# Feed-forward gate and up: one 512-column and one 256-column matmul in place of three of 256

## The reference

```python
D_MODEL, D_FF, SEQ = 1024, 2816, 256
for layer in range(2):
    h = rms_norm_3(x, ffn1_norm[layer])
    x = x + FFN_RES * swiglu(h, ffn1_w_gate[layer], ffn1_w_up[layer], ffn1_w_down[layer])
    ...   # pooling and convolution, or selected attention
    h = rms_norm_3(x, ffn2_norm[layer])
    x = x + FFN_RES * swiglu(h, ffn2_w_gate[layer], ffn2_w_up[layer], ffn2_w_down[layer])
# swiglu(h, g, u, d) = (silu(h @ g) * (h @ u)) @ d
```

## Time and profile before

| | us |
|---|---|
| median of 3 runs | 2860.81 |
| lowest, highest | 2857.11, 2861.9 |
| span of the profiled execution | 2859.0 |

### The profile page before, as it was taken

The page is one execution under the profiler, slowest core; times in us unless marked ns, Lnnn a source line. Parts: engine busy times, 40 slices in busy tenths (PEclk is TensorE's granted clock), DMA queues, the critical chain, the costliest instruction groups (busy, mean ns, idle before and its releaser), DMA issues. The chain is left out here.

```text
span 2859.0 us, 34779 instructions
## 1 busy us (share of the span) xinstructions
PE 2528.2 (88%) x14785; PEld 1811.3 (63%) x14785; DVE 1213.7 (42%) x1891; ACT 936.4 (33%) x1495; POOL 36.9 (1%) x51
## 2 busy tenths in 40 slices
PE   9898787767998889867978999999889999988998
PEld 7642222227742233217867777998779899887997
DVE  6520000026622000015665565655765565566654
ACT  5420000016510000013444434544544454434543
POOL 0010000000010000000000000000000000001000
PEclk9999999988999999998998999999999999999999
DMA  7099999993299999998222434555235555544452
GB/s 268 20 428 428 424 427 428 428 390 115 78 421 424 426 426 426 428 355 229 89 89 96 162 133 163 164 182 191 94 118 179 190 178 189 172 150 144 150 180 78
DMA packets 229162, 690.43 MB, mean 241 GB/s; under 512 B 35953, under 2 KB 135233, under 8 KB 205328
## 3 DMA queue, kind: packets, MB, share of 16 engines
q1 hardware_dynamic: 227728, 685.06, 64.0%
q0 software_dynamic: 1280, 3.15, 0.4%
HBM read 687.09 MB, written 5.28 MB: 242 GB/s over the span
## 5 line engine op out<-in xcount | busy, mean ns | idle before, releaser
L520 PE MATMUL accumulators<-xT_halves,weight_highs 128*128 128x256 f32 (+1 forms) x4400 | 812.7, 287 | 18.0 <-PEq L361 15.5
L267 DVE TENSOR_TENSOR weight_lows<-weight_ring,weight_highs 128x1024 fp32r<-128x1024 f32 (+1 forms) x504 | 602.9, 1213 | 435.5 <-ACT weight_highs L258 431.0
L520 PEld LDWEIGHTS accumulators<-xT_halves,weight_highs 128*128 128x128 f32 (+1 forms) x4400 | 693.5, 194 | 26.5 <-DVE weight_lows L267 14.4
L258 ACT CAST weight_highs<-weight_ring 128x1024 fp32r<-128x1024 f32 (+1 forms) x504 | 517.5, 1041 | 443.3 <-PE accumulators L520 424.9
L520 PE MATMUL accumulators<-xT_halves,weight_lows 128*128 128x256 f32 (+1 forms) x2200 | 628.0, 285 | 0.0
L1737 PE MATMUL accumulators<-weight_ring,arena 128*32 128x512 f32 x2048 | 471.8, 622 | 93.0 <-DMA weight_ring<-in_moe_w_up 50.7
L520 PEld LDWEIGHTS accumulators<-xT_halves,weight_lows 128*128 128x128 f32 (+1 forms) x2200 | 426.0, 194 | 0.5
L1737 PEld LDWEIGHTS accumulators<-weight_ring,arena 128*32 128x32 f32 x2048 | 135.6, 114 | 421.1 <-issue 420.9
L520 PE MATMUL accumulators<-weight_highs,arena_halves 128*128 128x512 f32 x1040 | 333.3, 398 | 12.4 <-PEq L361 5.4
L1737 PE MATMUL accumulators<-weight_ring,work 128*32 128x512 f32 x896 | 208.4, 620 | 34.8 <-DMA weight_ring<-in_moe_w_down 24.3
L520 PEld LDWEIGHTS accumulators<-weight_highs,arena_halves 128*128 128x128 f32 x1040 | 199.6, 192 | 57.5 <-issue 12.0
(11 more groups left out here) (441 smaller groups left out, 1970.7 us busy)
## 6 DMA issues: line engine op xcount, KB each, us to landing
weight_ring<-in_moe_w_gate SPq DMA_DIRECT2D x64, 2048.0 KB, 18.7
weight_ring<-in_moe_w_up SPq DMA_DIRECT2D x64, 2048.0 KB, 18.8
weight_ring<-in_moe_w_down SPq DMA_DIRECT2D x56, 2048.0 KB, 18.8
weight_ring<-in_ffn_w_gate SPq DMA_DIRECT2D x44, 1024.0 KB, 5.3
weight_ring<-in_ffn_w_up SPq DMA_DIRECT2D x44, 1024.0 KB, 5.3
weight_ring<-in_ffn_w_down SPq DMA_DIRECT2D x44, 1024.0 KB, 4.9
weight_ring<-in_l_w_in SPq DMA_DIRECT2D x38, 1024.0 KB, 5.1
weight_ring<-in_moe_w_down SPq DMA_DIRECT2D x32, 512.0 KB, 14.0
```

The source lines that it names most:

```text
L258: act.copy(p.high(), p.raw()).then_inc(self.high_ready, 1)
L267: dve.tensor_tensor(p.low(), p.raw(), p.high().bitcast(F32), ALU.subtract).then_inc(self.low_ready, 1)
L520: last = pe.matmul(out, left[a], right[b], start=(start and i == 0), stop=(stop and i == 2), **kw)
```

## The change

A group becomes two matmuls. The high weight tile streams the high and the low tokens in one matmul of 512 columns, into a bank of its own; the low weight tile streams the 256 high tokens into the first half of that bank. The two halves of a bank are then one sum in two parts: ScalarE copies the first half (two banks, 2 x 256 columns) to `gate` or `prod`, and VectorE adds the second half to it, and only then scales, or multiplies. Eight banks are in use in place of four, so TensorE waits in unit 1 for the row factors to have left bank 6, and before the down product for the sum of unit 9. ScalarE's new copies stand ahead of the Silu (gate) and at the end of the turn (up), each behind a wait for TensorE's last use of the part's weights; the cast of piece 4u + 7 moves from the next turn to before the up copy.

```diff
+    def bank(u, part, f):
+        return u % 2 * 4 + part * 2 + f
+
+    def sides(u, part):
+        acc = m.ps[:, bank(u, part, 0):bank(u, part, 0) + 2, :]
+        return acc[:, :, 0:T], acc[:, :, T:2 * T]
+
+    def two(x, u):
+        return x[:, u % 2, :].rearrange("p (f t) -> p f t", f=2)
 # TensorE
                     if u >= 2:
                         if part == 0:
-                            pe.wait_ge(s["scaled"], u - 1)
+                            pe.wait_ge(s["gate_summed"], u - 1)
                         else:
-                            pe.wait_ge(s["hidden"], u - 1)
+                            pe.wait_ge(s["up_summed"], u - 1)
+                    if (u, part) == (1, 1):
+                        pe.wait_ge(s["spread_moved"], 1)
...
                         for f in range(2):
-                            last = three(pe, acc[:, f * T:(f + 1) * T], [x[:, f * P:(f + 1) * P] for x in w], [m.xT_r[:, c, k, :] for k in range(2)],
-                                         f == 0 and c == 0, c == DC - 1, skip_group_check=True)
+                            high, low = (x[:, f * P:(f + 1) * P] for x in w)
+                            acc = m.ps[:, bank(u, part, f), :]
+                            pe.matmul(acc, high, m.xT_r[:, c, :, :].rearrange("p k t -> p (k t)"), start=(c == 0), stop=False, skip_group_check=True)
+                            last = pe.matmul(acc[:, 0:T], low, m.xT_r[:, c, 0, :], start=False, stop=(c == DC - 1), skip_group_check=True)
...
+            pe.wait_ge(s["up_summed"], n - 1)
             for i in range(FFC - 2):
                 out.chunk(pe, i)
 # ScalarE
             for u in range(n):
                 m.highs(act, gs.piece(4 * u + 2 + LEAD))
+                gs.wait_used(act, 2 * u)
+                if u == 0:
+                    act.wait_ge(s["spread"], 1)
+                if u >= 2:
+                    act.wait_ge(s["hidden"], u - 1)
+                act.copy(two(gate, u), sides(u, 0)[0]).then_inc(s["gate_copied"], 1)
                 act.wait_ge(s["scaled"], u + 1)
                 act.activation(gate[:, u % 2, :], gate[:, u % 2, :], ACT.Silu).then_inc(s["silu_out"], 1)
                 if u > 0:
                     rounded(u - 1)
+                m.highs(act, gs.piece(4 * u + 4 + LEAD) - 1)
+                gs.wait_used(act, 2 * u + 1)
+                if u >= 2:
+                    act.wait_ge(s["hidden_low"], u - 1)
+                act.copy(two(prod, u), sides(u, 1)[0]).then_inc(s["up_copied"], 1)
 # VectorE
-                gs.wait_used(dve, 2 * u)
-                dve.tensor_tensor(gate[:, u % 2, :].rearrange("p (j t) -> p j t", j=2), m.ps[:, u % 2 * 2, :].rearrange("p (j t) -> p j t", j=2),
-                                  bview(late.rows_of, 1, 2), ALU.mult).then_inc(s["scaled"], 1)
+                dve.wait_ge(s["gate_copied"], u + 1)
+                dve.tensor_tensor(two(gate, u), sides(u, 0)[1], two(gate, u), ALU.add).then_inc(s["gate_summed"], 1)
+                dve.wait_ge(s["gate_summed"], u + 1)
+                dve.tensor_tensor(two(gate, u), two(gate, u), bview(late.rows_of, 1, 2), ALU.mult).then_inc(s["scaled"], 1)
                 m.lows(dve, gs.piece(4 * u + 4 + LEAD) - 1)
-                gs.wait_used(dve, 2 * u + 1)
+                dve.wait_ge(s["up_copied"], u + 1)
+                dve.tensor_tensor(two(prod, u), sides(u, 1)[1], two(prod, u), ALU.add).then_inc(s["up_summed"], 1)
                 dve.wait_ge(s["silu_out"], u + 1)
-                if u >= 2:
-                    dve.wait_ge(s["hidden_low"], u - 1)
-                dve.tensor_tensor(prod[:, u % 2, :], gate[:, u % 2, :], m.ps[:, u % 2 * 2 + 1, :], ALU.mult).then_inc(s["hidden"], 1)
+                dve.wait_ge(s["up_summed"], u + 1)
+                dve.tensor_tensor(prod[:, u % 2, :], gate[:, u % 2, :], prod[:, u % 2, :], ALU.mult).then_inc(s["hidden"], 1)
```

More of the change, by code:

```diff
@@ L3340, in half @@
         return hT[:, k, 2 * u:2 * u + 2, :].rearrange("p c t -> p (c t)")
-    with m.stage("ffn", "silu_out", "hidden", "hidden_high", "hidden_low", "scaled", "spread", "spread_moved", *tail.names, joined=True) as (block, s):
+    def bank(u, part, f):
[5 more added lines that the diff above has]
+        return x[:, u % 2, :].rearrange("p (f t) -> p f t", f=2)
+    with m.stage("ffn", "silu_out", "gate_copied", "gate_summed", "up_copied", "up_summed", "hidden", "hidden_high", "hidden_low", "scaled", "spread", "spread_moved", *tail.names, joined=True) as (block, s):
         @block.sync
@@ L3353, in _ @@
                 for part in range(2):
-                    acc = m.ps[:, u % 2 * 2 + part, :]
                     pieces = gs.pieces[2 * u + part]
```

## The result

The changed kernel takes 2846.51 us (median of four runs, 2843.94 to 2849.01) against 2859.52 us for the kernel before (four runs, 2857.11 to 2861.9): a ratio of 0.9956, with a 95% interval of 0.9943 to 0.9968. It is 13.0 us faster. The forecast was 18.7 us and 2842.1 us: the direction is right and the time lies inside the range (2837 to 2849), but just outside the forecast's own range of 2839 to 2846. So there are two things to explain: why it is faster, and where some 5 us went.

What follows compares the result with a forecast made beforehand. The prediction took TensorE's unbroken matmul steps to bound the feed-forward stages: 13.3 ns saved in each of 1408 groups, 18.7 us taken, no added cost, so 2860.8 - 18.7 = 2842.1 us; own range 2839 to 2846, 8-in-10 range 2837 to 2849.

Steps and rivals of the forecast that it cites:

- What bounds the kernel: Four feed-forward stages: TensorE's matmul steps alone, without stalls; 180.80 us by steps against 180.82 in the chain.
- The fixed part of 13.3 ns a matmul: Gate and up: each matmul costs 13.3 ns beyond its columns; one fewer in each of 1408 groups saves 18.8 us.
- rival b: Gate and up: the wide matmul hides its weight load; 333.3 ns a group, 37.5 us gained, 2823 us; chance 0.03.
- rival (a): Gate and up: fixed part grows where narrow follows wide, the group stays at 360 ns; 2861 us, no change; chance 0.06.
- 346.7 ns if each step keeps the price of its own width: Gate and up: a group takes 226.7 + 120.0 ns in place of 360.0; upper end 348.5, gain then 16.2 us.
- the sum says 18.7: Whole kernel: 18.8 us from 1408 groups, under 0.1 us off for the slow clock in the first stage; no cost added.
- Scatter of 1 to 2 us: Whole kernel's time: allowance added to gains of 16.2 to 18.8 us, giving the forecast's own range, 2839 to 2846 us.
- ScalarE and VectorE: Gate and up: added copies and additions make 6.6 and 6.9 us of 11.5 a unit; cost taken: none.
- just in step: Gate and up: VectorE's shortest way round a unit, 11.1 us, equals TensorE's 11.1.
- The way round and its allowance: ScalarE and VectorE need 11.1 us a unit; 6.0 us of lag are covered at the down product's start.
- Rival (c): Gate and up: the hand-over between ScalarE and VectorE becomes the bound; 13 us slower, 2874 us; chance 0.04.
- Rival (d): Feed-forward stages: drift with a stall of 1 to 3 us each, or costly edges; 2846 to 2854 us; chance 0.09.

Runs made afterwards that it cites:

- a2_narrow: Changed kernel with the high weight tile streamed in two matmuls of 256 columns again, new banks, copies, additions and waits kept: 2861.8 us, ratio 1.0005 to the kernel before.
- b3_no_low: Changed kernel without the product of low weights and high tokens in gate and up, low tiles still made and waited for: 2780.8 us, a single run.
- b1_fill1: Changed kernel plus one VectorE operation in each unit of gate and up, writing scratch nobody reads: 2845.94 us, ratio 0.9953 to the kernel before.
- a3_gate_wide: Changed kernel with the wide matmul in gate only, up in three matmuls of 256 columns: 2849.47 us, ratio 0.9962 to the kernel before.
- b2_fill2: Changed kernel plus two VectorE operations in each unit of gate and up, writing scratch nobody reads: 2894.65 us, a single run.
- the c runs: c1_by_piece, c3_by_slice and c4_by_part: the changed kernel's matmuls in orders with fewer changes of width; 2848.04, 2849.38 and 2848.39 us.
- c4_by_part: Changed kernel with a part's sixteen high tiles streamed first, then its sixteen low tiles: 2848.39 us, ratio 0.9962 to the kernel before.
- c1_by_piece: Changed kernel with eight high tiles, then eight low tiles, in each piece of four slices: 2848.04 us, ratio 0.9958 to the kernel before.
- c3_by_slice: Changed kernel with two high tiles, then two low tiles, for each slice: 2849.38 us, a single run.

## Why the prediction was right, and where it missed

**What bounds the kernel: right.** A stage is TensorE's steps and nothing else. a2_narrow, with all the rest of the change in place, has the stages of before.

**The fixed part of 13.3 ns a matmul: right in 12 of 16 stages.** In the fast rhythm stages 2, 3 and 4 are 4.6, 4.6 and 4.7 us shorter, against 4.7 foretold, and the first 5.4 (its first microseconds at the lower clock scatter; the two profiles of the kernel before differ by 0.8 there). The pair's lower bound of 333 ns (rival b) and the 360 of rival (a) are out. The Trainium skill's formula (page "TensorE: Matmul & The Clock Gate", section "Back-to-back issue gap"), columns at 2.4 GHz and some 2.5 ns, which that section gives for a single matmul by itself and not for a stream of them with their weight loads, gave 2857.3 us; the trace disagrees with it here.

**"346.7 ns if each step keeps the price of its own width": this is the step that failed in size.** It holds in the fast rhythm only, and there as a sum: the steps are 230 to 232 and 115 to 117 ns and not 226.7 and 120, so only the sum is as foretold; why the two share it otherwise, no run shows. In the slow one a group costs 353, outside the 348.5 that I took as its upper end. I took that end from a single change of width in the trace of before, and a single one can't show a rhythm. The rows of before have no strict alternation, and I should have let the unknown reach halfway to rival (a), whose mechanism (the fixed part grows where a wide matmul is followed by a narrow one) is partly what happens: in the slow rhythm it is the wide step that is longer, 237 ns. Four slow stages in four profiles make 4 x 2.15 / 4 = 2.2 us a run. The four profiles of kernels with the whole change have 754.1 us in the stages on average, the three with narrow matmuls 771.0: a gain of 16.9 us, where the sum says 18.7.

**Scatter of 1 to 2 us: too small.** The other part of the first result was none of the change's. In that profile the untouched code took 2095.0 us, the most of all thirteen, against a mean of 2089. The clock there differs from execution to execution, and the whole time with it, by 6 to 8 us either way. Medians of four to six runs wander with it: 2846.5, 2842.2 and 2845.9 for one and the same kernel. The ratios 0.9944 and 0.9952 agree with 16.9 us (0.9941) inside their intervals, and 0.9956 falls just short (its interval begins at 0.9943). By the mean of the three ratios the gain is 14.1 us. Whether the 2.8 us between that and 16.9 are scatter, or the slow rhythm being commoner in the runs without a profile, these runs don't settle.

**ScalarE and VectorE: right.** VectorE in the kernel after, from the first low tile of a unit to its gate scaling, the stretch of the earlier trace rows (the last column is idle time and what ended it):

```profile
2158.84 1.23 DVE L267 TENSOR_TENSOR weight_lows<-weight_ring,weight_highs 128x1024 fp32r<-128x1024 f32 x1 [2.16 <-ACT weight_highs L258]
2160.81 0.69 DVE L3443 TENSOR_TENSOR work<-accumulators,work 128x512 f32<-128x512 f32 x1 [0.74 <-ACT work L3422]
...
2162.81 3.49 DVE L267 TENSOR_TENSOR weight_lows<-weight_ring,weight_highs 128x1024 fp32r<-128x1024 f32 x3
2166.35 0.69 DVE L3438 TENSOR_TENSOR work<-accumulators,work 128x512 f32<-128x512 f32 x1
2167.08 0.69 DVE L3440 TENSOR_TENSOR work<-work 128x512 f32<-128x512 f32 x1
```

and ScalarE's copies in the same unit, to be read beside the earlier trace rows:

```profile
2165.73 0.59 ACT L3413 COPY work<-accumulators 128x512 f32<-128x512 f32 x1 [1.66 <-PE accumulators L3384]
...
2171.28 0.59 ACT L3422 COPY work<-accumulators 128x512 f32<-128x512 f32 x1 [1.39 <-PE accumulators L3384]
```

The additions take 0.69 and the copies 0.59 us, as foretold. The gate addition starts at 2166.35; the third of the low tiles before it ends at 2166.30 (2162.81 + 3.49), and the copy it needs at 2166.32: VectorE is "just in step". The 0.74 us before the up addition is the only time in the unit that it loses to ScalarE's copies, which themselves wait for TensorE.

**The way round and its allowance: right in result, the way round 1 us too long.** I had 11.1 us for it; b3_no_low shows 10.12. I had 6.0 us of allowance at the start of the down product; the kernel after shows 5.7. With nothing added there is no lag at all, and the allowance is never touched. Rival (c) has a slip in its sum: six hand-overs at 0.3 us in place of 0.1 make a way round of 12.3 us, not 12.5, and by the prediction's own rule a loss of some 5 us in all, not 13. It was where I put it, at a chance of 0.04, and it takes 1.0 us a unit more of work on the way round to begin and, by b1_fill1, more than 1.2 to be paid for.

**Rival (d), a stall of 1 to 3 us in each stage, gave nearly the measured time for another reason.** There is no such stall: the idle time before L3383 is 1.4 us in four stages, and 0.5 us of it is the start of the second one, where the kernel before waits 0.5 us too. The first result alone, 2846.5 us, would have fitted (d) well; only the profile refutes it.

## What to carry to other kernels

Where TensorE is the bound without a gap, count instructions as well as columns: two matmuls with the same stationary tile merged into one of twice the columns gave 13 ns each here, if the accumulators have the banks and the evacuation lies beside other work. Price a new pattern of instruction widths with a wide upper bound until it has been run at length. And before a missing 0.2% is explained by the change, compare the untouched stretches of two profiles, since here they alone differed by up to 13.5 us.

## What the runs showed of the hardware that I had not expected

A strict alternation of 512 and 256 columns, each with a new 128x128 tile of weights, has two steady rhythms at a granted clock of 1.00: ten groups in 3.46 to 3.47 us or in 3.53. Unbroken, the alternation keeps its rhythm, as from a stage's second part to the down product. It takes one anew where it begins again: behind each part of narrow matmuls in a3_gate_wide, slow and fast in turn, and behind waits in b2_fill2 (second stage: ten groups in 3.47 us from 2165.25, in 3.54 from 2178.20, after a delay of some 0.1 us at 2177.4). Equal widths (a2_narrow, 120 ns) and blocks of equal widths (the c runs) showed one pace only. What decides which of the two it takes isn't shown by any run.

Blocks have a price too, but it does not go by the changes of width: in a part of 16 groups c4_by_part has 2 changes and takes 347.9 ns a group, c1_by_piece has 4 and takes 349.2, c3_by_slice has 16 and takes 348.3, and the fast alternation, with 32, takes 346.7.

A loop of the same instructions outside the change took 165.5 to 171.1 us from one execution to the next, with a mean granted clock of 0.95 to 0.92.
